# Order of the up products, the transposes and the weight splits in the expert stage of a two-block kernel

## The reference, cut to what matters

```python
def hierarchical_moe(h, w_rg, b_rg, w_re, b_re, w_gate, w_up, w_down):
    # top-1 group of 4, then top-2 of the 4 experts inside it: 16 experts of width 256
    ...
    a = jnp.einsum('td,edf->tef', ht, w_gate)
    u = jnp.einsum('td,edf->tef', ht, w_up)
    hid = jax.nn.silu(a) * u * combine[..., None].astype(ht.dtype)
    out = jnp.einsum('tef,efd->td', hid, w_down)
...
x = x + hierarchical_moe(rms_norm(x, ffn_norm_g), ...)
x = x + sigmoid(rms_norm(x, ple_norm_g) @ w_pg) * (p @ w_ple)
```

## Time and profile before

| | us |
|---|---|
| median of 3 runs | 771.78 |
| lowest, highest | 771.27, 772.0 |
| the profiled execution | 770.84 |
| its span | 769.1 |
| PE busy | 754.7 (98%) |
| DVE busy | 549.4 (71%) |
| ACT busy | 461.1 (60%) |

### The profile page before, as it was taken

How to read it: one execution, slowest core, us unless ns; L and a number is a source line. 1 busy time by engine, 2 the same in 40 slices (tenths; PEclk the granted TensorE clock), 3 DMA queues, 4 the chain that set the end, 5 groups by cost and what they waited for, 6 DMA issues and landing times.

```text
span 769.1 us, 12122 instructions
## 1 busy us (share of the span) xinstructions
PE 754.7 (98%) x4800; PEld 634.9 (83%) x4800; DVE 549.4 (71%) x674; ACT 461.1 (60%) x576; POOL 43.0 (6%) x80
## 2 busy tenths in 40 slices
PE   8999999999999999999999999999998999999988
PEld 8989878888998978888888998888876677878667
DVE  6898896575779697667578777358679656576765
ACT  7785596545587668554468635434566445465645
POOL 5500000000000000400000001000021000000000
PEclk9999999999999999999999999999999999999999
DMA  8666244555446435466645345644059589989901
GB/s 277 195 221 216 84 163 143 194 181 195 137 138 221 164 112 180 149 205 167 223 130 180 131 159 170 207 175 165 1 164 406 213 308 325 368 289 411 330 32 55
DMA packets 70040, 149.60 MB, mean 195 GB/s; under 512 B 8458, under 2 KB 11104, under 8 KB 69984
## 3 DMA queue, kind: packets, MB, share of 16 engines
q1 hardware_dynamic: 69568, 148.78, 56.0%
q0 software_dynamic: 384, 0.04, 0.3%
q10 hardware_dynamic: 32, 0.01, 0.0%
HBM read 147.76 MB, written 1.05 MB: 193 GB/s over the span
## 4 chain that ended last, share of the span: by engine, by line
PE 92%; DVE 3%; DMA 2%; ACT 1%; issue 1%; SPq 0%; POOL 0%; DVEq 0%; ACTq 0%; POOLq 0%
PE mm L760 18%; PE mm L761 18%; PE mm L762 18%; PE mm L776 4%; PE mm L777 4%; PE mm L778 4%; PE aux L871 3%; PE aux L1317 3%; PE aux L1316 3%; PE aux L1318 3%; PE aux L1301 2%; DVE sb_w_lo L1961 2%; DMA sb_raw<-in_w_up 2%; PE aux L760 1%; PE aux L762 1%; PE aux L761 1%
## 5 line engine op out<-in xcount | busy, mean ns | idle before, releaser
L1961 DVE TENSOR_TENSOR sb_w_lo<-sb_raw,sb_w_hi 128x2048 fp32r<-128x2048 f32 (+2 forms) x135 | 277.2, 2064 | 70.3 <-ACT sb_w_hi L1444 41.5
L1444 ACT ACTIVATE sb_w_hi<-sb_raw 128x2048 fp32r<-128x2048 f32 (+1 forms) x83 | 155.3, 1871 | 117.9 <-PE mm L762 87.9
L760 PE MATMUL mm<-sb_w_hi,sb_hT_hi 128*128 128x512 f32 (+1 forms) x456 | 175.9, 386 | 0.0
L761 PE MATMUL mm<-sb_w_lo,sb_hT_hi 128*128 128x512 f32 (+1 forms) x456 | 172.7, 379 | 0.0
L762 PE MATMUL mm<-sb_w_hi,sb_hT_lo 128*128 128x512 f32 (+1 forms) x456 | 172.6, 379 | 0.0
L760 PEld LDWEIGHTS mm<-sb_w_hi,sb_hT_hi 128*128 128x128 f32 x456 | 85.8, 188 | 17.5 <-issue 2.0
L762 PEld LDWEIGHTS mm<-sb_w_hi,sb_hT_lo 128*128 128x128 f32 x456 | 85.8, 188 | 16.4
L761 PEld LDWEIGHTS mm<-sb_w_lo,sb_hT_hi 128*128 128x128 f32 x456 | 85.9, 188 | 14.9
L776 PE MATMUL mm<-sb_hT_hi,sb_w_hi 128*128 128x256 f32 x272 | 78.3, 288 | 0.0
L777 PE MATMUL mm<-sb_hT_lo,sb_w_hi 128*128 128x256 f32 x272 | 76.9, 283 | 0.0
L778 PE MATMUL mm<-sb_hT_hi,sb_w_lo 128*128 128x256 f32 x272 | 76.9, 283 | 0.0
(11 more groups left out here) (461 smaller groups left out, 1145.9 us busy)
## 6 DMA issues: line engine op xcount, KB each, us to landing
sb_raw<-in_w_in SPq DMA_DIRECT2D x120, 512.0 KB, 4.6
sb_raw<-in_w_gate SPq DMA_DIRECT2D x30, 512.0 KB, 8.2
sb_raw<-in_w_up SPq DMA_DIRECT2D x30, 512.0 KB, 10.3
sb_raw<-in_w_down SPq DMA_DIRECT2D x18, 512.0 KB, 9.8
sb_raw<-in_w_out SPq DMA_DIRECT2D x16, 512.0 KB, 4.3
sb_pg_t<-in_w_down SPq DMA_DIRECT2D x14, 512.0 KB, 8.8
...
```

Of the source, the lines that this page charges most:

```text
L760: pe.matmul(dst, a_hi, rhs[0], start=start, stop=False, skip_group_check=True)
L761: pe.matmul(dst, a_hi, rhs[1], start=False, stop=False, skip_group_check=True)
L1444: act.activation(w_hi[:, t % RING, 0:width], raw[:, t % RING, 0:width], ACT.Copy).then_inc(hi_split, 1)
L1961: return dve.tensor_tensor(out_, a, b, op)
```

## The change

1. **TensorE's order.** Per step now U0.s, U1.s, `hidden_T(s-1)`, `down(s-2)`.
2. **Split counts of their own.** Instead of one table there are four: how many high parts ScalarE has made before `silu(s)` and before `eT_high(s-1)`, and how many low parts VectorE has made before `hidden(s)` and before `eT_rest(s-1)`. On both engines the turn of `silu(s)` or `hidden(s)` now comes ahead of that of `eT(s-1)`.
3. **Slot numbers later.** The product L1271 leaves `slot_products`, becomes `slot_rows` in another PSUM bank and runs ahead of U0.13; `pick_T` follows it, and `scatter` waits for it, no longer `down(0)`.
4. **The end.** On ScalarE the split of TG goes ahead of `eT_high(15)`, that of TG + 1 ahead of `y_high(1, 0)`, that of TG + 2 behind the eight scalings. On VectorE the low part of TG + 1 goes from ahead of the first `add_piece` to behind the last, and `y_low(1, 1)` behind the first `add_piece`.
5. **The first tile's up columns.** ScalarE's queue issues them: ScalarE reads the expert's number (a `value_load` that waits for `order_ready`) and issues two DMAs ahead of the two copies of `ple` sums out of PSUM (`sb_pl_t`), which TensorE waits for in the gather. SP keeps the two gate DMAs.

```diff
-SPLITS_BEFORE = [5, 7, 8, 10, 12, 14, 15, 18, 20, 23, 25, 27, 31, 32, 34, 36]
+HIGHS_BEFORE_SILU = [4, 6, 9, 10, 13, 15, 15, 19, 21, 23, 26, 27, 32, 34, 36, 38]
+HIGHS_BEFORE_TURNED = [4, 6, 9, 10, 14, 15, 17, 19, 22, 23, 27, 31, 32, 35, 36, 38]
+LOWS_BEFORE_HIDDEN = [4, 6, 8, 10, 13, 13, 16, 18, 20, 23, 26, 28, 30, 33, 34, 37]
+LOWS_BEFORE_TURNED = [4, 6, 8, 10, 13, 14, 16, 18, 22, 24, 26, 29, 32, 34, 35, 37]
+ROWS_STEP = 13
...
             for s in range(STEPS):
                 if s == 1:
                     slot_products()
+                if s == ROWS_STEP:
+                    slot_rows()
                 up(s, 0)
-                if s >= 2:
+                up(s, 1)
+                if s >= 1:
                     hidden_T(s - 1)
-                up(s, 1)
-                if s == 1:
-                    hidden_T(0)
                 if s >= 2:
                     down(s - 2)
...
+            act.wait_ge(S["order_ready"], 1)
+            first = act.value_load(order_i[0:1, column(0):column(0) + 1], min_val=0, max_val=EXPERTS - 1)
+            act.wait_ge(lo_split, RING + raw_before(TM + 1) + 1)
...
+            for second in range(2):
+                c = slice(second * W, (second + 1) * W)
+                act.dma_start(dst[:, c], src[:, c]).then_inc(raw_loaded[raw_slot(TM + 1)] if second else S["half_loaded0"], 16)
             for c in range(2):
                 if c == 0:
                     act.wait_ge(S["ple_done"], 1)
...
             for s in range(1, STEPS):
-                done = hi_until(s, done)
+                highs(HIGHS_BEFORE_TURNED[s - 1], HIGHS_BEFORE_SILU[s])
+                silu(s)
+                highs(HIGHS_BEFORE_SILU[s], HIGHS_BEFORE_TURNED[s])
                 eT_high(s - 1)
-                silu(s)
-            hi_late(AT_TILE["down", STEPS - 2])
-            hi_late(AT_TILE["down", STEPS - 1])
+            hi_late(TG)
             eT_high(STEPS - 1)
             for c in range(2):
                 y_high(0, c)
-            hi_late(TG)
+            hi_late(TG + 1)
             act.wait_ge(S["y_half"], 1)
             y_high(1, 0)
             act.wait_ge(tile_done, RING + AT_TILE["down", 15] + 1)
             y_high(1, 1)
-            hi_late(TG + 1)
-            hi_late(TG + 2)
             for kk in range(KT):
...
+            hi_late(TG + 2)
             hi_late(TG + 3)
...
             for s in range(1, STEPS):
-                done = low_until(s, done)
+                lows(LOWS_BEFORE_TURNED[s - 1], LOWS_BEFORE_HIDDEN[s])
+                hidden(s)
+                lows(LOWS_BEFORE_HIDDEN[s], LOWS_BEFORE_TURNED[s])
                 eT_rest(s - 1)
-                hidden(s)
...
-            split_low(AT_TILE["down", STEPS - 2])
+            split_low(AT_TILE["down", STEPS - 1])
             eT_rest(STEPS - 1)
-            split_low(AT_TILE["down", STEPS - 1])
             for c in range(2):
                 y_low(0, c)
             split_low(TG)
-            for c in range(2):
-                y_low(1, c)
-            split_low(TG + 1)
+            y_low(1, 0)
...
             add_piece(0, 0)
+            y_low(1, 1)
             add_piece(0, 1)
...
             add_piece(1, 1)
+            split_low(TG + 1)
             for kk in range(4, 8):
                 tail_low(kk)
```

More of the change, by code:

```diff
@@ L1266, in slot_products @@
             def slot_products():
-                pe.wait_ge(S["slot_diag_ready"], 1)
                 pe.wait_ge(S["weights_ready"], 1)
-                for tt in range(TT):
-                    pe.matmul(mm[0][:, tt * P:(tt + 1) * P], ones[:], diag[:, tt, :], start=True, stop=True)
                 for rows_, c in ((slice(0, 64), slice(192, 256)), (slice(64, P), slice(0, 64))):
```

39 lines of the change are left out of this document (23 added, 16 removed).

## The result

| | before | changed |
|---|---|---|
| median | 771.52 us (4 runs, 770.82 to 772.0) | 760.77 us (4 runs, 760.48 to 761.04) |
| the profiled execution | 770.84 | 761.01 |
| its span | 769.1 | 759.3 |
| PE busy | 754.7 (98%) | 751.1 (99%) |

The changed kernel takes 0.9861 of the time (95% interval 0.9844 to 0.9878): 10.75 us, or 1.4%, less. The forecast was 8.7 us less: 763.1 us, with a range from 761.3 up. The direction was right, the gain was put too small, and the result lies 0.5 us under the range.

A forecast was written before the change was run, and what follows sets the result against it. TensorE, busy 98% of the span, bounds the kernel, so only its waits and slow clock, 9.7 us, could be won. Terms -5.2 + 0.3 + 0.5 - 1.8 - 2.5 + 0 = -8.7 took 771.78 to 763.1 us, range 761.3 to 767.3.

The forecast's parts named there:

- term 1: Stall at step 2: the new order shortens TensorE's waits and avoids the low clock, U0.3 starts at 602.4, -5.2 us.
- Terms 2 and 3: Steady steps: U1.13's high part delays eT_high(10), +0.3 us (0 to 3); L1271 uncovered ahead of U0.13, +0.5 us.
- Term 4: D.14: its high and low parts come earlier, so TensorE's wait goes, -1.8 us; 0 if loads are late.
- Term 5: Tail, from D.15's end to the first product with w_pg: 4.9 us instead of 7.4, -2.5 us.
- The walk through step 2: Event times of VectorE, ScalarE and TensorE in the new order, with two TensorE waits of 0.5 us and no clock dip.
- the one tight place that is over: Steps 3 to 14: tightest places keep 0.4 us slack; U1.13's high part plus eT_high(10) need some 3.0 against 2.8 us.
- rival in the middle: New waits at steps 8 to 13, 766 us, chance 0.20; or step 2's stall stays in part, 768 us, chance 0.10.
- I take 0: First tile's up columns by ScalarE's queue: no net effect, bounds -0.8 and +1.3 us.
- no wait over 0.7 us between 571 us and the tail: Sign that the forecast is right: TensorE has no longer wait than 0.7 us in that stretch.
- third rival: The second queue fills the DMA engines: all landings 0.8 us earlier, 762.3 us, chance 0.07.
- TensorE does the same matmuls: Steady steps: moving hidden_T past an up tile leaves TensorE's work unchanged; costs were sought on the other engines.
- tenths at seams: Small remainder added, unpriced, to the 9.7 us of TensorE waits and slow clock that could be won.

The follow-up runs named there:

- e1: Changed kernel with SyncE's queue again issuing the first tile's up columns instead of ScalarE's: 760.49 us.
- e3: Changed kernel with the old order of steps 1 and 2 alone (split counts, turns of eT, place of step 1's transposes): 766.23 us.
- e2: Changed kernel with the transposes put back between the two up tiles in the five steps with whole up tiles: 764.38 us.
- e8: Changed kernel with SyncE held until the first half of U0.0 has landed before it issues the next tile's loads: 762.12 us.
- e6: Kernel before with the transposes moved behind both up tiles in the five steps with whole up tiles, nothing else changed: 769.26 us.
- e12: Kernel before with ScalarE's queue issuing the first tile's up columns, nothing else changed: 772.33 us, ratio 1.0002 to 1.0020.
- e4: Changed kernel with the old tail: splits of TG to TG + 2 and y_low(1, 1) in their old places: 764.23 us.
- e5: Kernel before with 16 extra small matmuls filling TensorE's wait ahead of step 1's transposes: 768.12 us.

## Why the prediction was right and wrong

| step | forecast | profiled |
|---|---|---|
| 1, stall at step 2 | -5.2 | -5.3 |
| 2 and 3, U1.13's high part ahead of `eT_high(10)`, L1271 ahead of U0.13 | +0.8 | +0.7 |
| 4, D.14 | -1.8 | -1.9 |
| 5, tail | -2.5 | -2.7 |
| ScalarE's queue | 0 (-0.8 to +1.3) | +0.8 |
| breaks in the whole tiles | not in the sum | -1.6 |
| start of the gather, run to run | not in the sum | +0.2 |
| sum | -8.7 | -9.8 |
| from profiled executions to medians | not in the sum | -0.9 in the medians |

The profiled column is worked out from the table of differences: U0.3 moved by 4.39 although U0.0 was 0.95 late, so term 1 is 4.39 + 0.95; of the 0.95 the gather's start has 0.18 and the queue 0.77. Terms 2 and 3 are U0.12 to U0.13, 698.11 - 688.98 = 9.13 us against 703.10 - 694.69 = 8.41. Term 4 is 7.17 - 5.31. Term 5 is 4.74 us against 7.41 from D.15's end to the product. The breaks are five times 0.33. That the queue's 0.77 us reach U0.3 in full is read from e1: with SyncE's queue U0.0 to U0.3 takes 31.1 us there, as in the changed kernel (31.0). The sum, 9.8, is what lies between the two profiled executions (9.83).

**Right.** The walk through step 2 gave the right order of events and, without the queue, the right size; e3 brought the stall back alone. The first L1312 was due at about 602.4 us and came at 603.28, by the queue's lateness. D.14 without a wait, the tail in 4.74 us for 4.9, U1.13 as the one tight place that is over, TG + 2's low part not waited for, the clock at 1.00: all as said. No rival in the middle came true (one wait of 0.17 us for `eT` in step 11 is all); e2 shows that a part of it would have, had only half of the reorder been made.

**Wrong, first: the edit costed at nothing.** "I take 0" stood on two legs: the half that ScalarE waits for would gain, and VectorE's chain behind U0.0 would cover the rest. The half landed later, and there was no cover: TensorE runs from U0.0 to U0.1 without a wait. I watched the wrong place for it; the first gather matmul (567.00, not later than 567.5) was fine, U0.0 was 0.77 us late behind it, and its wait of 1.19 us, up to 572.26, breaks the sign "no wait over 0.7 us between 571 us and the tail". The Trainium skill, "Trainium Kernel Development and Optimization" (Key Constraints), says that issuing from several engines saves only issue time. The runs agree as far as nothing was gained, and go further: here it cost 0.3 to 1.0 us by the medians. The saved issue time brought the next tile's load forward, onto this one's (e8); how much the closer issue of the four pieces adds is not shown. The third rival, which filled the DMA engines by a second queue, falls with it.

**Wrong, second: "TensorE does the same matmuls".** That sentence, under the steady steps, priced the move of `hidden_T` at nothing, and put "tenths at seams" aside as part of what could be won without asking how many. The rows of the kernel before held most of the number: two groups of 16 with the transposes between them take 4.13 us up to the down product, and each group of 16 takes 1.88 up to what follows, so 0.37 go to two transposes. What the same work costs without the break (3.80) only e6 and the changed kernel show. Five steps of 0.33 us is more than terms 2 and 3 together.

**Wrong, third: the step from one execution to the median.** The forecast subtracted the profile's terms from the median as if the difference of 0.94 us between the two were the same in both kernels. It was not: the old kernel's median lies 0.7 to 0.9 us above its profiled execution, the changed kernel's 0.2 below. The profile showed one stretch of low clock, and by their mean clocks most runs of the old kernel had more. The wait of 2.5 us in the tail was priced at 2.5; in e12's profile 1.5 us of clock follow it. A hint stood in the table of times, since all three timed runs lay above the profiled one; the changed kernel's lie around its own.

The first two partly cancel (+0.8, -1.6): with the profiled differences in place of the forecast ones the sum gives 771.78 - 9.83 = 762.0 us, inside the range. Another 0.26 is that the median of before came out at 771.52 with the fourth run, and the third step's 0.92 puts the result 0.5 us below the range. The breaks alone would have sufficed as well: with their 1.6 us not won it would have been 762.4. That the range was missed by 0.5 us and not met is in part luck; that 1.6 us were missing from the sum is not.

**Open.** Why the same wait in the tail is followed by the low clock in some runs and not in others (e4: two of five); why e5, which left that wait in place, had 1.000 in all five, and e3, which has not got it, down to 0.994; what made four of e3's runs 2 us longer than the profiled one; where e12 lost its 0.8 us; and differences of up to 1.2 us in the gather's start between profiles (566.35 to 567.52), which lies ahead of all that was changed.
